# Sums of squares of the HGRN heads from a high and a low part in fp32r

## The reference, cut to what matters

```python
def rms_norm(x, gain):
    xf = x.astype(jnp.float32)
    y = xf * lax.rsqrt(jnp.mean(xf * xf, axis=-1, keepdims=True) + NORM_EPS)
    return (y * gain.astype(jnp.float32)).astype(x.dtype)
...
    o_c = hgrn2_mixer(c_q, c_f, c_i, lbs[l])
    o_c = rms_norm(o_c, hgrn_norm[l].reshape(HG_HEADS, HG_VDIM)).reshape(B, T, C_WIDTH) * jax.nn.silu(c_silu)
```

## Time and profile before

| | us |
|---|---|
| median of 3 runs | 485.43 |
| lowest, highest | 485.16, 486.59 |
| profiled execution, its own time | 485.57 |
| its span, first to last instruction | 483.8 |
| PE busy | 475.2 (98%) |
| DVE busy | 343.2 (71%) |
| ACT busy | 264.6 (55%) |
| POOL busy | 159.1 (33%) |

### The profile page before, as it was taken

How to read it: one execution, slowest core, us unless ns; L and a number is a source line. 1 busy time by engine, 2 the same in 40 slices (tenths; PEclk the granted TensorE clock), 3 DMA queues, 4 the chain that set the end, 5 groups by cost and what they waited for, 6 DMA issues and landing times.

```text
span 483.8 us, 9621 instructions
## 1 busy us (share of the span) xinstructions
PE 475.2 (98%) x3948; PEld 463.9 (96%) x3948; DVE 343.2 (71%) x577; ACT 264.6 (55%) x398; POOL 159.1 (33%) x157
## 2 busy tenths in 40 slices
PE   9999999999999999899999999999999999999995
PEld 8999999999999999889999999999999999999995
DVE  4898967798976566797896747878584257655653
ACT  6887744594562737553565346576554245433531
POOL 1074820807100009990256415436745120000000
PEclk9999999999999999999999999999999999999999
DMA  8956634454354755555355343253525536677502
GB/s 297 330 170 192 189 103 143 125 171 142 119 175 122 188 137 166 155 164 184 119 187 162 106 133 113 87 156 107 174 89 173 175 120 192 213 233 246 175 1 87
DMA packets 76006, 76.43 MB, mean 158 GB/s; under 512 B 5759, under 2 KB 74751, under 8 KB 75963
## 3 DMA queue, kind: packets, MB, share of 16 engines
q1 hardware_dynamic: 75675, 75.64, 50.4%
q10 hardware_dynamic: 288, 0.18, 0.2%
HBM read 74.77 MB, written 1.05 MB: 157 GB/s over the span
## 4 chain that ended last, share of the span: by engine, by line
PE 94%; DVE 2%; ACT 2%; issue 1%; DVEq 0%; ACTq 0%
PE ps L997 75%; PE ps L1022 4%; PE ps L1160 3%; PE ps L1111 2%; PE ps L1185 1%; PE ps L1100 1%; PE ps L1179 1%; PE ps L1127 1%; DVE WL L629 1%; PE ps L1023 1%; PE ps L1114 1%; PE ps L1038 1%; PE ps L1129 1%; PE ps L1128 1%; PE ps L1065 1%
## 5 line engine op out<-in xcount | busy, mean ns | idle before, releaser
L997 PE MATMUL ps<-hH,WL 128*128 128x256 f32 x688 | 195.6, 288 | 1.2 <-DVE WL L629 1.2
L997 PE MATMUL ps<-hL,WH 128*128 128x256 f32 x688 | 194.8, 284 | 0.0
L997 PE MATMUL ps<-hH,WH 128*128 128x256 f32 x688 | 194.8, 284 | 0.0
L629 DVE TENSOR_TENSOR WL<-W,WH 128x2048 fp32r<-128x2048 f32 (+1 forms) x66 | 152.9, 2317 | 19.5 <-PE ps L997 17.1
L432 ACT ACTIVATE WH<-W 128x2048 fp32r<-128x2048 f32 (+1 forms) x66 | 124.7, 1889 | 47.9 <-PE ps L997 46.6
L997 PEld LDWEIGHTS ps<-hH,WL 128*128 128x128 f32 x688 | 130.6, 191 | 2.3 <-DVE WL L629 1.4
L997 PEld LDWEIGHTS ps<-hL,WH 128*128 128x128 f32 x688 | 131.8, 192 | 0.8 <-issue 0.7
L997 PEld LDWEIGHTS ps<-hH,WH 128*128 128x128 f32 x688 | 131.7, 191 | 0.0
L394 POOL TENSOR_SCALAR R<-R,st 128x256 f32<-128x256 f32 x32 | 29.2, 924 | 82.1 <-DVE st L804 82.1
L997 PE MATMUL ps<-bH,WL 128*128 128x256 f32 x192 | 54.9, 286 | 0.0
L997 PE MATMUL ps<-bH,WH 128*128 128x256 f32 x192 | 54.3, 283 | 0.0
(11 more groups left out here) (192 smaller groups left out, 779.3 us busy)
## 6 DMA issues: line engine op xcount, KB each, us to landing
W<-w_in SPq DMA_DIRECT2D x48, 1024.0 KB, 5.2
W<-w_branch SPq DMA_DIRECT2D x12, 1024.0 KB, 5.3
W<-w_out SPq DMA_DIRECT2D x4, 1024.0 KB, 5.4
W<-w_in SPq DMA_DIRECT2D x2, 608.0 KB, 3.8
R<-x SPq DMA_DIRECT2D x2, 512.0 KB, 4.6
W<-w_in SPq DMA_DIRECT2D x2, 512.0 KB, 6.7
R<-cmp_w SPq DMA_DIRECT2D x2, 512.0 KB, 8.5
OC<-pool_w SPq DMA_DIRECT2D x4, 256.0 KB, 5.9
```

Of the source, the lines that this page charges most:

```text
L629: dve.tensor_tensor(slab_view(WL[:, s % 2], s), slab_view(W[:, s % 3], s), slab_view(WH[:, s % 3], s), ALU.subtract).then_inc(s_lo, 1)
L997: mm = pe.matmul(o, l, r, start=(at == 0 if mixed else k0 + k == 0 and j == 0), stop=(at == len(order) - 1 if mixed else k0 + k == KC - 1 ...
```

## The change

ACT now forms each head's squares twice from the same PSUM: once in fp32 (`SQ`, as before) and once rounded to fp32r (`SQH`). DVE subtracts the two for a pair of heads (`SQL`, fp32r) in slabs 13, 17, 21 and 25 (`SQL_AT`). PE takes two fp32r matmuls of 512 columns into the same PSUM bank in place of one fp32 matmul, with a matrix of ones in fp32r (`ONE`) that DVE copies once near the start. PE waits for `s_sql` in place of `s_hsq`. `SQH` and `SQL` lie over buffers that are not in use then (`PT1`, half of `BR`).

```diff
+SQL_AT = tuple(U0 + 4 + 4 * p for p in range(HG // 2))
...
                     if s == U0 + 2 + 2 * h:
                         act.wait_ge(s_hpv, 2 * h + 2)
                         act.wait_ge(s_scan, h // 2 + 1)
+                        if h >= 2:
+                            act.wait_ge(s_sql, h // 2)
                         act.activation(SQ[:, h % 2], ps[:, 6, 0:T], ACT.Square).then_inc(s_hsq, 1)
+                        if h >= 2:
+                            act.wait_ge(s_hss, h // 2)
+                        act.activation(SQH[:, h % 2], ps[:, 6, 0:T], ACT.Square).then_inc(s_sqh, 1)
                         act.activation(OC[:, h, :], ps[:, 6, 0:T], ACT.Copy).then_inc(s_hoc, 1)
...
                         dve.tensor_tensor(sq_, sq_, HQ[:, h], ALU.mult).then_inc(s_hmul, 1)
+                for p in range(HG // 2):
+                    if s == SQL_AT[p]:
+                        dve.wait_ge(s_hsq, 2 * p + 2)
+                        dve.wait_ge(s_sqh, 2 * p + 2)
+                        if p:
+                            dve.wait_ge(s_hss, p)
+                        dve.tensor_tensor(SQL.rearrange("p e t -> p (e t)"), SQ.rearrange("p e t -> p (e t)"),
+                                          SQH.rearrange("p e t -> p (e t)"), ALU.subtract).then_inc(s_sql, 1)
...
             dve.tensor_copy(MB[:], causal)
+            dve.tensor_copy(ONE[:], ones).then_inc(s_one, 1)
...
                     if s == U0 + 5 + 4 * p:
-                        pe.wait_ge(s_hsq, 2 * p + 2)
+                        pe.wait_ge(s_one, 1)
+                        pe.wait_ge(s_sql, p + 1)
                         if p:
                             pe.wait_ge(s_hrs, p)
-                        pe.matmul(ps[:, 7, :], ones, SQ.rearrange("p e t -> p (e t)"), start=True,
+                        pe.matmul(ps[:, 7, :], ONE[:], SQH.rearrange("p e t -> p (e t)"), start=True, stop=False)
+                        pe.matmul(ps[:, 7, :], ONE[:], SQL.rearrange("p e t -> p (e t)"), start=False,
                                   stop=True).then_inc(s_hss, 1)
```

More of the change, by code:

```diff
@@ L131, in trunk @@
         PM = sb("PM", [P, 2, 640])
+        with nc.sbuf_tensor("SQH", [P, 2, T], F32R) as SQH:
+            pass
         PT1 = sb("PT1", [P, 768])
         CP = sb("CP", [P, 2048])
+        with nc.sbuf_tensor("rho_place", [P, 512], F32), nc.sbuf_tensor("SQL", [P, 2, T], F32R) as SQL:
+            pass
         BR = sb("BR", [P, 2, 512])
@@ L141, in trunk @@
         MB = sb("MB", [P, P])
+        ONE = sb("ONE", [P, P], F32R)
         GT = sb("GT", [P, TT, GATES])
@@ L222, in trunk @@
         s_hoc, s_hn = sem("hg_out"), sem("hg_normed")
+        s_sqh, s_sql, s_one = sem("hg_sq_hi"), sem("hg_sq_lo"), sem("ones_ready")
         s_ckh, s_ck, s_cv = sem("ck_hi"), sem("ck_lo"), sem("cv_out")
```

## The result

| | before | changed |
|---|---|---|
| median, us | 485.44 (6 runs) | 490.6 (6 runs) |
| lowest, highest | 485.16, 486.59 | 489.47, 491.19 |
| profiled execution, span | 485.57, 483.8 | 491.19, 489.3 |

The ratio of changed to before is 1.0099, with a 95% interval of 1.0082 to 1.0116: slower by 5 us, where 2.6 us was forecast. The direction was right, the size was double, and the time lies above the stated range of 485.4 to 490.0 us.

What follows compares the result with a forecast made beforehand. The prediction took PE to set the pace between 1 and 478 us. Its terms 2.99 - 0.03 - 0.39 + 0 gave +2.57 us, so 485.43 became a median of 488.0 us, with a range of 485.4 to 490.0 us.

Steps and rivals of the forecast that it cites:

- What bounds the kernel; what PE saves: PE sets the pace between 1 and 478 us; two fp32r matmuls save 0.39 us per pair if PE doesn't wait.
- Pair 0: Slab 14: PE idles 3.14 us for DVE's subtraction, which stands behind seven products; +2.99 us.
- Pairs 1, 2, 3: Slabs 18, 22, 26: -0.03 us (wait eats saving), -0.39 us (no wait), 0 (saving lost in later PE waits).
- ACT, DVE, the copy of the ones: Eight extra ACT squares, later DVE work and one DVE copy fit into idle time: 0, bounds 0 to +0.3 us.
- Rival 1: Slab 14: the clock falls in PE's 3.14 us gap, costing 3.2 us more: 491.2 us, or 489.6; chance 0.15.
- the sum: Whole kernel: 2.99 - 0.03 - 0.39 + 0 = +2.57 us, median 488.0 us.
- the sign that the prediction itself named: Slab 14's product starting at half clock, listed among the things that would show the forecast wrong.
- The half price: Clock fall at slab 14 with a climb half as long as 3.2 us: 489.6 us.
- the full price: Clock fall at slab 14 with the whole 3.2 us climb from rest: 488.0 + 3.2 = 491.2 us.
- Rival 2: Slab 13: DVE's six products take 1.3 us, not 3.64, if POOL is past its pieces; gap 0.8, 485.7 us; chance 0.08.
- Rival 3: PE's waits at 202 and 209 us don't hang on PE and give back 2.16 us: 485.8 us; chance 0.08.
- Rival 4: Slab 14: subtraction done before PE comes, no gap, only savings: 484.3 us, or 483.9 with the fourth saving; chance 0.06.

Runs made afterwards that it cites:

- the filled gap: Changed kernel plus 12 fp32r filler matmuls on PE before its wait for pair 0's low part: 487.7 to 488.2 us in five executions, 489.25 in one.
- the last experiment on it: Kernel with the subtraction ahead of the products, pair 3's sum left as one fp32 matmul: 484.1 to 484.2 us (7 executions), 485.6 to 485.7 (5).

## Why the prediction was wrong

**What bounds the kernel; what PE saves.** Right. Two fp32r matmuls cost 0.46 us in the chain where nothing is waited for, the fp32 one 0.86.

**Pair 0.** The order on DVE, the start of the subtraction (98.87 forecast, 98.91 measured), its 0.69 us (0.68) and the gap (3.14, measured 3.2) were right. From the end of the subtraction to the matmul it took 0.14 us, not 0.06. The 2.99 us were right as the price of the wait: the filled gap measured the whole sum at 2.7 against 2.57. What was missing in this term is that PE comes out of the gap at half clock: +0.48 for the two matmuls and +0.95 for the product.

**Pairs 1, 2, 3.** Right: offsets of 0, -0.39 and 0 between the traces. Pair 3's saving became waiting time, as the last experiment on it shows.

**ACT, DVE, the copy of the ones.** Right at 0.

**The rivals.** Rival 1 was what happened. The step that failed is the sum, which has no term for the clock and takes it as 1.00 behind the gap; the fall was left to a rival at 0.15. What the runs showed in its place is a fall at slab 14 of 1.4 to 1.5 us, and the sign that the prediction itself named, slab 14's product at half clock. That fall alone gives some 489.5 us, still inside the range; the second fall, in four of six executions, took the median to 490.6, above 490.0, and for it the prediction has no term either. The row for the first fall was in hand: at the end of the trace the clock fell 3.1 us after PE's last matmul, and the gap forecast was 3.14 us. Against it stood only that gaps of 1.21 and 0.95 us brought no fall in one execution, which says nothing of a gap of 3.1. Its price was too high on the other hand: 3.2 us from the start of the kernel, where 1.4 to 1.5 us was measured; why the start costs more no run shows. The half price that was mentioned, 489.6, was about right for one fall. That the full price gave 491.2, near the slowest executions, is luck: those have two falls.

**The table of times.** The 486.59 among three runs of the kernel before was not scatter. By its time it was the second level, one fall, 1.1 to 1.4 us above the others. Its mean clock, and the rows of such an execution, would have shown that even waits of about 1 us each can bring the clock down in this kernel, and that 488.0 had to be widened by one fall upward on that account alone.

Rivals 2, 3 and 4 did not happen. Rival 2's mechanism is real, but POOL was where it had been; taking it away gave a gap of 1.4 us, not 0.8: the six products still took 1.82 us against 1.29 in slab 17, and the POOL operation ahead of the two that were taken out still ran beside them until 95.29.

## What to carry to other kernels

A matmul made cheaper by work on another engine is worth its saving only if that work stands early in the other engine's queue: here moving one instruction ahead of seven turned +4.2 us into -1.0. A wait of PE costs its length and, from some 2 us on in these runs, often also a spell at half clock, so a new gap is priced with both, or filled with matmuls that need no new wait. Where the times of an unchanged kernel stand at two levels, look at the mean granted clock of each before calling it scatter, and compare equal levels.

## What the runs showed of the hardware

- A fall keeps the granted clock at 0.50 for some 3.4 us (99.6 to 103.0 and 215.6 to 219.0 in the changed kernel) and costs 1.4 to 1.5 us at slab 14. Near 216 it costs 1.4 us in the trace and 1.3 us between the levels of the kernel before.
- It need not come while PE is idle: near 216 it came 1.5 to 2.3 us after PE had started again, in the five traces that have it.
- By times and clocks it came behind the gap in all four executions with 2.6 us and in at least four of six with 3.2 us, in one of four with 2.2 us, in six of twelve with 2.0 us (the filler in bank 7), in none of four with 1.3 us. The Trainium skill, TensorE: Matmul & The Clock Gate, section HAM oscillation — how this bites in real kernels, warns only of gaps longer than these; the runs decide, and shorter ones were enough.
- Shorter idle times near each other bring it too: 1.21 and 0.95 us, 7 us apart, in 30 of 68 executions of the kernel before, and 0.56, 0.97 and 0.95 us within 15 us in 18 of 33 (the subtraction ahead, POOL quiet, pair 0 in fp32). With 12 or 8 fillers at slab 14 and the same later waits it was one of ten; why it is rarer there is not shown.
- The two POOL operations of 1.15 us that read SBUF made two of DVE's two-input operations four times as long (0.28 to 1.19 us); a memset on POOL did not.
